# Differential attention on one core: 40 units in one sequence, score products from 64-row tiles, a bias table for each head

## What is computed

```python
slopes = 2.0 ** (-8.0 * arange(1, 5) / 4)             # 1/4, 1/16, 1/64, 1/256
def block(q_blk, i):                                  # 128 queries, 4 heads, 2 maps of width 64
    s = einsum('bqhmd,bkhmd->bhmqk', q_blk, k) * 64 ** -0.5
    bias = -slopes * abs(qpos[:, None] - kpos[None, :])
    p = softmax(s + bias, axis=-1)
    pd = p[:, :, 0] - lam * p[:, :, 1]
    return einsum('bhqk,bkhe->bqhe', pd, v)           # v has width 128 for each head
o = rmsnorm(o, subln_g) * (1.0 - lambda_init)
```

## Time and profile before

| what | us |
|---|---|
| median of 3 runs (3053.56 to 3060.9) | 3055.45 |
| the profiled execution | 3056.16 |
| span of the profiled execution | 3054.3 |
| TensorE busy in the span | 2750.1 (90%) |
| VectorE busy | 1995.9 (65%) |
| ScalarE busy | 1438.8 (47%) |

### The profile page before, as it was taken

How to read it: one execution, slowest core, us unless ns; L and a number is a source line. 1 busy time by engine, 2 the same in 40 slices (tenths; PEclk the granted TensorE clock), 3 DMA queues, 4 the chain that set the end, 5 groups by cost and what they waited for, 6 DMA issues and landing times. The chain is left out here.

```text
span 3054.3 us, 90989 instructions
## 1 busy us (share of the span) xinstructions
PE 2750.1 (90%) x39070; PEld 2130.6 (70%) x39070; DVE 1995.9 (65%) x3188; ACT 1438.8 (47%) x2171; POOL 321.0 (11%) x260
## 2 busy tenths in 40 slices
PE   5999988996999999955934999999999999999994
PEld 3455544665999999942524777888877777788872
DVE  3344077776565455434268888888888888888883
ACT  3211155664222222222223666666666666666663
POOL 0000000002113112213200100111111000011000
PEclk8999999997999999977966999999999999999997
DMA  4113141002112112033315999999999999999984
GB/s 129 34 37 142 27 193 67 0 0 77 52 51 74 52 45 80 11 147 110 124 41 203 308 307 333 312 311 318 309 316 308 309 300 314 320 319 309 315 278 154
DMA packets 282900, 544.78 MB, mean 178 GB/s; under 512 B 13296, under 2 KB 96880, under 8 KB 282576
## 3 DMA queue, kind: packets, MB, share of 16 engines
q1 hardware_dynamic: 273728, 505.62, 48.1%
q0 software_dynamic: 8848, 34.08, 4.3%
HBM read 487.23 MB, written 52.43 MB: 177 GB/s over the span
## 5 line engine op out<-in xcount | busy, mean ns | idle before, releaser
L1677 DVE SCALAR_TENSOR_TENSOR arena<-arena 128x1024 f16<-128x1024 f32 x768 | 904.2, 1221 | 95.2 <-ACT arena L1622 95.0
L1576 PE MATMUL ps<-arena 128*128 128x160 f16 x12288 | 854.4, 233 | 8.2 <-DVE arena L1686 3.3
L1576 PEld LDWEIGHTS ps<-arena 128*128 128x128 f16 x12288 | 850.8, 98 | 12.8 <-issue 9.6
L1622 ACT ACTIVATE arena<-arena 128x1024 f16<-128x1024 f32 x768 | 766.7, 1049 | 145.3 <-PE ps L1601 144.9
L897 PE MATMUL ps<-arena 64*64 64x32 f32 (+2 forms) x14080 | 501.5, 224 | 22.4 <-DVEq L1062 21.2
L897 PEld LDWEIGHTS ps<-arena 64*64 64x64 f32 x14080 | 481.5, 135 | 28.5 <-DVEq L1062 21.4
L1593 PE MATMUL ps<-arena 128*128 128x512 f16 x1536 | 363.6, 388 | 0.0
L389 PE MATMUL ps<-arena 128*128 128x512 f16 (+1 forms) x1584 | 285.7, 344 | 0.7 <-ACT arena L235 0.7
L1593 PEld LDWEIGHTS ps<-arena 128*128 128x128 f16 x1536 | 142.3, 99 | 182.8 <-issue 36.4
L389 PEld LDWEIGHTS ps<-arena 128*128 128x128 f16 x1584 | 154.9, 98 | 131.7 <-ACT arena L235 1.2
L1643 ACT ACTIVATE arena<-ps 128x160 f32<-128x160 f32 x256 | 77.7, 304 | 256.8 <-PE ps L1576 256.6
(11 more groups left out here) (219 smaller groups left out, 2911.0 us busy)
## 6 DMA issues: line engine op xcount, KB each, us to landing
arena<-w_gate SPq DMA_DIRECT2D x128, 1024.0 KB, 5.1
arena<-w_up SPq DMA_DIRECT2D x128, 1024.0 KB, 5.6
arena<-w_down SPq DMA_DIRECT2D x128, 1024.0 KB, 6.5
arena<-feat SPq DMA_DIRECT2D x120, 256.0 KB, 4.7
feat<-arena SPq DMA_DIRECT2D x20, 640.0 KB, 3.0
arena<-w_in SPq DMA_DIRECT2D x21, 512.0 KB, 3.9
arena<-tokens SPq DMA_DIRECT2D x20, 512.0 KB, 4.1
feat<-arena POOLq DMA_DIRECT2D x1, 7680.0 KB, 22.8
```

The costliest lines, as they stand in the source:

```text
L1576: ins = pe.matmul(ps[:, o:o + SLOTS], part(4 * c + 2 * w + k // 4, pw) [:, k % 4, f * P:(f + 1) * P], xT2[:, px, k], start=(k == 0 and i = ...
L1622: act.activation(split[k % SPLIT][:, q * PW:(q + 1) * PW], ring[k % RING][:, q * PW:(q + 1) * PW], ACT.Copy, scale=W_SCALE).then_inc(w_hi, 1)
L1677: v.scalar_tensor_tensor(split[k % SPLIT][:, WCH + q * PW:WCH + (q + 1) * PW], ring[k % RING][:, q * PW:(q + 1) * PW], W_SCALE, split[k % ...
```

## The change

- `keep_qk` is written out and multiplies the four q tiles by 0.125 as it moves them. `qz`, its clearing, its filling and the wait for it are gone.
- `scores` takes 64 rows of `qk` for each map, rows 0 to 63 for map 0 and 64 to 127 for map 1, as both operands. For long units the order is now: first 512 keys of map 0, of map 1, last 512 keys of map 0, of map 1. The waits for `scores_read` stand before the first piece of each map.
- `units` has all 40 units, head after head, and the loops over heads are written out as one pipeline. `keep_turned` has a new wait, for `o_psum` of two units before.
- The host gives four bias tables, each with its head's slope. They are loaded by four transfers of SyncE at the start of the attention block, the first with a semaphore of its own, and the load in the block before and the multiplications by 0.25 are gone. VectorE waits for the first table before its first unit and for the other three before head 1.
- In the tail TensorE transposes up to four outputs into one bank, and ScalarE copies them back together: 12 groups for 40 outputs.

The diff, cut; the functions that it replaces stand in the kernel above.

```diff
@@ -100,6 +100,7 @@
 
         F16 = mybir.dt.float16
         W_SCALE = 256.0
+        Q_SCALE = 0.125
         PRODUCTS = ((0, 0), (0, 1), (1, 0))
 
         A_, B_, C_, D_ = 0, 10240, 20480, 25600
@@ -262,15 +263,12 @@
                     act.wait_ge(proj_psum, 2 * j + (ZT + b + 1))
                     if more:
                         weights_hi(j + (ZT // 2 + 1), b)
-                    act.activation(qk[:, ds(2 * j + b, 1), :].rearrange("p a b -> p (a b)"),
-                                   ps[:, b * 2048:b * 2048 + NT],
-                                   ACT.Copy, scale=1.0 / W_SCALE).then_inc(proj_out, 1)
-
-                with act.Fori(0, 3) as j:
-                    for b in range(2):
-                        keep_qk(j, b, True)
-                for b in range(2):
-                    keep_qk(3, b, False)
+                    act.activation(qk[:, 2 * j + b, :], ps[:, b * 2048:b * 2048 + NT], ACT.Copy,
+                                   scale=(Q_SCALE if 2 * j + b < HEADS_A else 1.0) / W_SCALE).then_inc(proj_out, 1)
+
+                for j in range(4):
+                    for b in range(2):
+                        keep_qk(j, b, j < 3)
...
@@ -438,7 +434,6 @@
         with nc.Block() as block:
             @block.sync
             def _(sp):
-                sp.dma_start(bias, c_bias).then_inc(bias_in, 16)
                 sp.wait_ge(loraw_zero, 1)
...
-        qz = at(D_, 2, NT)
+        bias = [at(E_ + 2 * KD * P, BIAS_W)] + [at(A_ + 4096 + h * BIAS_W, BIAS_W) for h in range(HEADS_A - 1)]
+        assert 4096 + (HEADS_A - 1) * BIAS_W <= B_ - A_
+        bias_in = sem("bias_in")
+        more_bias_in = sem("more_bias_in")
         sc = at(D_ + 2 * NT, 2, 2, T0)
         pd = at(D_ + 2 * NT + 4 * T0, 2, T0)
...
+        units = [(h, t0, n, i) for h in range(HEADS_A) for t0, n in ((0, T0), (T0, T1)) for i in range(n // P)]
+        NU = len(units)
+        TAIL = [(h, u, min(4, NTT - u)) for h in range(HEADS_A) for u in range(0, NTT, 4)]
+            @block.sync
+            def _(sp):
+                for h in range(HEADS_A):
+                    sp.dma_start(bias[h], c_bias[:, h * BIAS_W:(h + 1) * BIAS_W]
+                                 ).then_inc(more_bias_in if h else bias_in, 16)
...
+                def scores(u):
+                    h, t0, n, i = units[u]
+                    w = min(512, n)
+                    for o in range(0, n, w):
                         for m in range(2):
+                            if u and o == 0:
+                                pe.wait_ge(scores_read, 2 * u + m - 1)
+                            rows = slice(64 * m, 64 * m + 64)
+                            ins = pe.matmul(ps[:, m * T0 + o:m * T0 + o + w],
+                                            qk[rows, h, t0 + i * P:t0 + (i + 1) * P],
+                                            qk[rows, HEADS_A + h, t0 + o:t0 + o + w], start=True, stop=True)
+                            if o + w == n:
+                                ins.then_inc(scores_psum, 1)
+
+                def turn(u):
+                    n = units[u][2]
+                    pe.wait_ge(pd_ready, u + 1)
+                    if u:
+                        pe.wait_ge(pdT_ready, u)
+                    for k in range(n // P):
+                        ins = pe.transpose(ps[:, 4 * 512 + k * P:4 * 512 + (k + 1) * P],
+                                           pd[:, u % 2, k * P:(k + 1) * P], ident[:, :])
+                    ins.then_inc(pdT_psum, 1)
+
+                def weigh(u):
+                    h, t0, n, i = units[u]
+                    pe.wait_ge(pdT_ready, u + 1)
+                    if u >= 2:
+                        pe.wait_ge(o_read, u - 1)
+                    for k in range(n // P):
+                        ins = pe.matmul(bank(6 + u % 2, P), pdT[:, u % 2, k, :],
+                                        vt[:, t0 // P + k, h * P:(h + 1) * P],
+                                        start=(k == 0), stop=(k == n // P - 1))
+                    ins.then_inc(o_psum, 1)
+
+                for s in range(NU + 3):
+                    if s < NU:
+                        scores(s)
+                    if 2 <= s < NU + 2:
+                        turn(s - 2)
+                    if s >= 3:
+                        weigh(s - 3)
+
+                for g, (h, u, w) in enumerate(TAIL):
+                    if g >= 4:
+                        pe.wait_ge(oT_read, g - 3)
+                    for q in range(w):
+                        pe.wait_ge(on_ready, h * NTT + u + q + 1)
+                        ins = pe.transpose(ps[:, (g % 4) * 512 + q * P:(g % 4) * 512 + (q + 1) * P],
+                                           oraw[:, h, u + q], ident[:, :])
+                    ins.then_inc(oT_psum, 1)
...
+                def keep_turned(u):
+                    n = units[u][2]
+                    act.wait_ge(pdT_psum, u + 1)
+                    if u >= 2:
+                        act.wait_ge(o_psum, u - 1)
+                    act.copy(pdT[:, u % 2, 0:n // P, :].rearrange("p a b -> p (a b)"),
+                             ps[:, 4 * 512:4 * 512 + n]).then_inc(pdT_ready, 1)
...
+                for g, (h, u, w) in enumerate(TAIL):
+                    act.wait_ge(oT_psum, g + 1)
+                    act.copy(qk[:, h, u * P:(u + w) * P], bank(g % 4, w * P)).then_inc(oT_read, 1)
...
-                v.memset(qz.rearrange("p a b -> p (a b)"), 0.0)
-                v.drain().then_inc(scores_read, 2)
-                        v.tensor_scalar(qz[64 * m:64 * m + 64, m, :],
-                                        qk[64 * m:64 * m + 64, ds(h, 1), :].rearrange("p a b -> p (a b)"),
-                                        0.125, None, ALU.mult)
-                    v.drain().then_inc(q_ready, 1)
-                    v.tensor_scalar(bias, bias, 0.25, None, ALU.mult)
-                    v.wait_ge(pdT_psum, NU * h + NU)
...
+                def biased(u):
+                    h, t0, n, i = units[u]
+                    if u == 0:
+                        v.wait_ge(bias_in, 16)
+                    if u == NTT:
+                        v.wait_ge(more_bias_in, 16 * (HEADS_A - 1))
                     for m in range(2):
+                        v.wait_ge(scores_psum, 2 * u + m + 1)
+                        v.tensor_copy(carry[0:1, 0:1], carry[0:1, 1:2])
+                        w = T0 - P - i * P
+                        v.tensor_tensor_reduce(sc[:, u % 2, m, 0:n], ps[:, m * T0:m * T0 + n],
+                                               bias[h][:, w:w + n], 1.0, -3.0e38, ALU.add, ALU.max,
+                                               small[:, 24 + m:25 + m])
+                        v.drain()
+                        v.tensor_scalar(srow[:, u % NR, m:m + 1], small[:, 24 + m:25 + m], -1.0, None,
+                                        ALU.mult).then_inc(scores_read, 1)
...
-        "c_bias": -dist,
+        "c_bias": np.concatenate([-dist * 0.25 ** (h + 1) for h in range(4)], axis=1),
```

More of the change, by code:

```diff
@@ new lines, in probs @@
+                def probs(u):
+                    n = units[u][2]
+                    for m in range(2):
+                        act.wait_ge(scores_read, 2 * u + m + 1)
+                        act.activation(sc[:, u % 2, m, 0:n], sc[:, u % 2, m, 0:n], ACT.Exp,
+                                       bias=srow[:, u % NR, m:m + 1],
+                                       accum_out=srow[:, u % NR, 2 + m:3 + m]).then_inc(probs_ready, 1)
+                def keep_turned(u):
+                    n = units[u][2]
+                    act.wait_ge(pdT_psum, u + 1)
[3 more added lines that the diff above has]
+                             ps[:, 4 * 512:4 * 512 + n]).then_inc(pdT_ready, 1)
@@ new lines, in keep_output @@
+                def keep_output(u):
+                    h, t0, _, i = units[u]
+                    act.wait_ge(o_psum, u + 1)
+                    o = oraw[:, h, t0 // P + i]
+                    act.activation(o, bank(6 + u % 2, P), ACT.Copy, scale=srow[:, u % NR, 4:5])
+                    act.drain().then_inc(o_read, 1)
+                    act.activation(ojunk, o, ACT.Square, accum_out=ostat[:, 0, u:u + 1])
+                for s in range(NU + 3):
+                    if s < NU:
+                        probs(s)
+                    if 2 <= s < NU + 2:
+                        keep_turned(s - 2)
+                    if s >= 3:
+                        keep_output(s - 3)
@@ new lines, in difference @@
+                def difference(u):
+                    n = units[u][2]
+                    v.wait_ge(probs_ready, 2 * u + 2)
+                    r = srow[:, u % NR]
+                    v.reciprocal(r[:, 4:6], r[:, 2:4])
+                    v.drain()
+                    v.scalar_tensor_tensor(r[:, 5:6], r[:, 5:6], cst[:, 2:3], r[:, 2:3], ALU.mult, ALU.mult)
+                    v.drain()
+                    if u >= 2:
+                        v.wait_ge(pdT_psum, u - 1)
```

(12 more changed lines are left out.)

82 lines of the change are left out of this document (removed).

## The result

The changed kernel takes 3111.05 us (median of 4 runs, 3105.91 to 3114.54) beside 3058.18 for the kernel before: ratio 1.0174, 95% interval 1.0152 to 1.0197. It is **53 us slower**, where I forecast 3025, some 31 us faster than before. The profiled execution took 3111.43 us, with a span of 3109.6.

What follows compares the result with a forecast made beforehand. PE bounds attention before, DVE after: 483.7 start + 41.2 first head + 3 x 46.9 heads + 3.5 + 8.5 + 14.0 = 691.6, against 722.87, 31.3 us earlier. 3056.2 - 31.3 = 3024.9, forecast 3025, range 3017 to 3041.

Steps and rivals of the forecast that it cites:

- All that follows is behind the barrier and moves along.: After attention: the mixer starts 31.3 us earlier and everything behind it shifts equally, 3056.2 to 3024.9 us.
- my rival on the slower side: Attention's long units: PE's pauses drop the clock to 1.2 GHz; 3091 us with 16 such units, chance 0.05.
- first head: Attention's start up to unit 8: 38.7 us plus 2.5 for a cold clock, 41.2.
- a head: Each later head: 14.8 us of DVE work, 2.5 waiting for PE, six long units at 4.94, together 46.9.
- Scores from tiles: Scores in a long unit: two 64-row tiles run abreast, 3.44 us falls to 1.72; each tile switch adds 0.15.
- rows 9: Mixer profile rows: float32 passes on alternating 64-row tiles take 57 ns each, where one alone would need 107.
- The fifth pass: Scores in a long unit: if the last pass runs alone, 2.15 us instead of 1.72, the upper bound.
- The long unit: Attention's long units: DVE becomes the bound at 4.91 us against PE's 4.67; taken as 4.94 a unit.
- Tables not shared evenly: Attention's start: first bias table lands in 5.2 us; four tables sharing the engines evenly would cost up to 6 more.
- Tail: Attention's end: DVE's scalings, 10.59 of 13.9 us, cover transposes and copies, so grouping gains nothing: 14.0.
- Rivals 1 to 3: Attention: row tiles don't overlap, 3057, chance 0.09; weight loads between passes, 3038, 0.06; clock falls, 3091, 0.05.
- Rival 2: Scores: each of four pass pairs waits for its weight load, 2.48 us, long unit 5.43; 3038 us, chance 0.06.

Runs made afterwards that it cites:

- slots 30 and 128: Head of TensorE's expert loop pinned at that slot of its 256-instruction block: changed kernel 3028.64 and 3111.02 us, kernel before 3059.47 and 3140.99.
- the branch without a hint: Kernel before, expert loop's head at slot 30, TensorE's loop without its hint_back_edge instruction: 3138.95 us, ratio 1.0281.
- four versions that differ in slot or order of passes alone: Changed kernel with the expert loop's head at slot 30, 176, 30 with each map's score passes together, and 100: 3028.64, 3024.02, 3023.23, 3028.57 us.
- 30 and 100: Changed kernel with the head of TensorE's expert loop pinned at slot 30 or 100 of its 256-instruction block: 3028.64 us (0.9900) and 3028.57 us (0.9912).
- slot 232: Changed kernel with the head of TensorE's expert loop pinned at slot 232 of its 256-instruction block: 3074.52 us, ratio 1.0074.
- slot 176: Changed kernel with the head of TensorE's expert loop pinned at slot 176 of its 256-instruction block: 3024.02 us, ratio 0.9901.

## Why the prediction was wrong, point by point

**The step that failed** is the sentence "All that follows is behind the barrier and moves along." I took it as safe since nothing behind the attention block is edited and all data dependencies end at the barrier. What crosses the barrier is the length of the program: 1,634 more instructions on TensorE moved its expert loop by 98 slots, and each turn lost 6.0 us. The sentence put what follows at nothing, where a term of 84 us was due. The runs at slots 30 and 128, of both kernels, show it. None of my rivals had it; my rival on the slower side was another mechanism.

What could have warned me: the change writes four heads out on TensorE ahead of a long hardware loop, and the trace of before had the price of a healthy branch, 0.36 us. The Trainium skill (Runtime: NRT & Kernel Launch, Instruction fetch mechanics) says that TensorE's instruction memory holds 2,048 instructions and is refilled in sequence in blocks of 256, and that a taken branch whose target isn't in the current window (of two blocks, it says) forces a fetch before execution goes on. The loop has 2,186 instructions, more than either, so by the section its head isn't held at the foot. The traces agree, with 4.35 us for the branch without a hint. The section doesn't tell of the hint or of the slot, which decide here between 0.36 and 4.3 us.

**Right, by its own steps.**

| step | forecast | measured |
|---|---|---|
| stage start to first read of VectorE | 5.2 | 4.7 |
| first head | 41.2 | 40.1 |
| a head | 46.9 | 47.3 |
| last two short units | 3.5 | 4.0 |
| last read to table load | 8.5 | 8.1 |
| tail | 14.0 | 14.0 |
| stage | 213.1 | 213.1 |

- *Scores from tiles*: four pass lengths, 1.72, and two switches of 0.15 make 2.02; measured 2.00 from the first score pass to the first transpose (499.43 to 501.43). The tiles do run abreast, and rows 9 were the right bound. The fifth pass (2.15) comes nearer in every other unit (2.21), where map 1's passes start 0.2 later.
- *The long unit*: forecast 4.94 by VectorE. The six steps from unit 12 to 18 of a head take 29.7, as forecast (29.6), but two errors cancel. VectorE's own unit is 4.78, not 4.91, and TensorE's is 4.78 too (forecast 4.67). What I had at nothing is `keep_turned`: ScalarE's copy of the turned probabilities (L661) is 0.28 late in every other settled unit, which with map 1's late start costs 0.5 in two of the six, and 1.30 late in a head's first short unit.
- *First head*: I added 2.5 for a cold clock. TensorE did pause and fall (a piece of eight passes took 5.20 at 482.48), and the head was still 1.1 shorter than forecast.
- *Tables not shared evenly*: the first landed 4.8 after its issue, so the 6 us of the range were not needed. The slowest of the four took 10.4, and nothing waited for it.
- *Tail*: 10.59 of VectorE's scalings again; the grouped transposes brought nothing, as forecast (14.0, and 13.9 before).
- *Rivals 1 to 3*: no unit of 6.4, none of 5.4, and a granted clock of 0.97 over the attention pipeline. Rival 2's rule, that loads of the same row group stand between passes, is not what this trace shows: loads hid beside the passes.

With the loop at a harmless place the kernel takes 3028.64, 3024.02, 3023.23 and 3028.57 in four versions that differ in slot or order of passes alone, all 0.990 or 0.991 of before: 26 to 29 us, of the 31 forecast. Each of these beats both kernels.

## What to carry to other kernels

A change's cost can lie where its diff isn't: code written out ahead of a long hardware loop (here 2,186 instructions; no run tried a shorter one) shifts where that loop falls, and a block's edge close ahead of its foot or close behind its head costs 3.4 to 6 us a turn, the clock included. After any change of a program's length, compare the duration of the loops' branches and the idle time put down to "issue" before judging the change itself, and pin the head, or try two or three slots clear of both edges (30 and 100 here). And a saving per unit counts only in the units where the faster engine had been the bound.

## What the runs showed of the hardware that I had not expected

- The same loop, the same hint: 0.36 us a branch with the foot at slots 114 to 238 of its block, 0.61 at 58, 4.3 at 10. Without a hint 4.35 at slot 168.
- With the head 24 instructions from its block's end, a stall of 2.2 to 2.9 us behind the head, in every turn; with 80 instructions one of 0.2 to 0.5; with 156 none.
- The pause at the foot costs more than its length: after it the granted clock falls to 0.50 for a while, 1.65 us on top of 3.95. At slot 232 the shorter stalls were followed by such a loss in five turns of 14.
- The clock also falls without any pause: behind the transposes of an expert the first twelve products of 512 columns take up to 4.45 us instead of 2.76, in 6 of 14 turns of the kernel before, in 10 of the kernel after, in none at slot 176. What decides it is open; it is worth up to 1.7 us a turn.
- TensorE doesn't keep the program's order between row tiles: eight passes on two tiles take 2.00 us, in pairs 6 to 7 ns apart when the program has them in turn and 12 to 14 ns apart when it has one tile's first.
- Also open: the order of the fetches behind the dear branch, and how near to a block's start a foot may come. Slots 10 and 58 were tried, nothing between.
